# Two-block transformer kernel on one core: the experts' input is normalised in place and gathered by every fourth column, and two weight rows of layer 0 take the place of the reordered copy

## What is computed

```
x = layer_norm(ALPHA * x + m, ln1_g[layer], ln1_b[layer])
f = moe(x, w_router, b_router, moe_w1[layer], moe_w3[layer], moe_w2[layer])
x = layer_norm(ALPHA * x + f, ln2_g[layer], ln2_b[layer])

# moe: each token goes to 2 of 16 experts; for an expert e and its tokens xb
hb = jax.nn.silu(xb @ w1[e]) * (xb @ w3[e])
y  = hb @ w2[e]
```

## Time and profile before

| what | value |
| --- | --- |
| time, median of 3 runs | 2213.72 us (2211.26 to 2217.29) |
| profiled execution, its own time | 2218.69 us |
| its span | 2217.0 us |
| instructions in the profile | 27358 |
| TensorE matmul busy | 2137.2 us, 96% |
| VectorE / ScalarE / GpSimd busy | 1048.4 / 757.4 / 98.3 us |
| mean granted clock of TensorE | 0.995 |
| moved by DMA | 618.28 MB, 279 GB/s over the span |

### The profile page before, as it was taken

How to read it: one execution, slowest core, us unless ns; L and a number is a source line. 1 busy time by engine, 2 the same in 40 slices (tenths; PEclk the granted TensorE clock), 3 DMA queues, 4 the chain that set the end, 5 groups by cost and what they waited for, 6 DMA issues and landing times.

```text
span 2217.0 us, 27358 instructions
## 1 busy us (share of the span) xinstructions
PE 2137.2 (96%) x10936; PEld 1419.2 (64%) x10936; DVE 1048.4 (47%) x1570; ACT 757.4 (34%) x1085; POOL 98.3 (4%) x107
## 2 busy tenths in 40 slices
PE   8999999998999999998889999999999999989999
PEld 6653334333585344333268888878888888878887
DVE  5720000001482000000167778768778776866776
ACT  4622111100362111111043346653344335555332
POOL 3300000000000000000000003000000000300000
PEclk9999999999999999999999999999999999989999
DMA  8599999999949999999975554245555554415551
GB/s 288 216 394 428 427 427 429 426 428 425 377 192 414 426 427 428 427 428 427 421 267 191 196 171 160 77 149 186 199 171 174 195 197 158 136 48 188 186 195 57
DMA packets 171255, 618.28 MB, mean 279 GB/s; under 512 B 7976, under 2 KB 116688, under 8 KB 147600
## 3 DMA queue, kind: packets, MB, share of 16 engines
q1 hardware_dynamic: 168688, 612.00, 71.3%
q0 software_dynamic: 2464, 4.84, 0.7%
HBM read 615.76 MB, written 1.05 MB: 278 GB/s over the span
## 4 chain that ended last, share of the span: by engine, by line
PE 77%; DMA 11%; DVE 5%; ACT 4%; DVEq 1%; SPq 1%; issue 1%; ACTq 0%
PE W L2225 22%; PE W L2487 12%; PE W L2488 6%; DMA moe_split<-in_moe_w 4%; PE acc L2087 4%; PE acc L2091 4%; PE acc L2088 4%; PE W L2059 3%; PE W L2061 3%; PE W L2060 3%; DMA moe_own<-in_moe_w 3%; PE W L2207 2%; DMA moe_raw<-in_moe_w 2%; DMA moe_xt<-in_moe_w 2%; PE acc L2216 2%; PE W L2491 2%
## 5 line engine op out<-in xcount | busy, mean ns | idle before, releaser
L1329 DVE TENSOR_TENSOR w_lo<-raw,w_hi 128x2048 fp32r<-128x2048 f32 (+2 forms) x198 | 433.8, 2194 | 158.6 <-ACT w_hi L830 150.2
L830 ACT ACTIVATE w_hi<-raw 128x2048 fp32r<-128x2048 f32 (+2 forms) x203 | 372.2, 1833 | 304.2 <-PE acc L2091 134.1
L2487 PE MATMUL W<-xT_both,w_hi 128*128 128x512 f32 x1218 | 438.0, 399 | 3.9 <-DVE xT_both L1347 3.1
L1599 DVE TENSOR_TENSOR hid<-W,hid 128x512 f32<-128x512 f32 x32 | 22.1, 692 | 717.5 <-PE W L2225 717.4
L2488 PE MATMUL W<-xT_both,w_lo 128*128 128x256 f32 x1218 | 341.7, 281 | 0.0
L2487 PEld LDWEIGHTS W<-xT_both,w_hi 128*128 128x128 f32 x1218 | 229.2, 188 | 55.2 <-issue 3.7
L2488 PEld LDWEIGHTS W<-xT_both,w_lo 128*128 128x128 f32 x1218 | 230.1, 189 | 7.0
L2225 PE MATMUL W<-moe_split,xe 128*64 128x512 f32 x672 | 150.2, 595 | 9.1 <-DMA moe_split<-in_moe_w 9.1
L2225 PE MATMUL W<-moe_own,xe 128*64 128x512 f32 x608 | 138.2, 601 | 8.0 <-DMA moe_own<-in_moe_w 8.0
L2059 PE MATMUL W<-w_hi,xT_both 128*128 128x474 f32 (+1 forms) x376 | 145.4, 387 | 0.0
L2061 PE MATMUL W<-w_hi,xT_both 128*128 128x474 f32 (+1 forms) x376 | 142.7, 379 | 0.0
(11 more groups left out here) (420 smaller groups left out, 2959.2 us busy)
## 6 DMA issues: line engine op xcount, KB each, us to landing
moe_split<-in_moe_w SPq DMA_DIRECT2D x60, 2048.0 KB, 26.4
moe_raw<-in_moe_w SPq DMA_DIRECT2D x54, 2048.0 KB, 27.6
moe_own<-in_moe_w SPq DMA_DIRECT2D x50, 2048.0 KB, 25.8
raw<-in_ffn_w_gate SPq DMA_DIRECT2D x44, 1024.0 KB, 5.2
raw<-in_ffn_w_up SPq DMA_DIRECT2D x44, 1024.0 KB, 5.1
raw<-in_ffn_w_down SPq DMA_DIRECT2D x44, 1024.0 KB, 4.9
moe_xt<-in_moe_w SPq DMA_DIRECT2D x18, 2048.0 KB, 30.5
raw<-in_w_in SPq DMA_DIRECT2D x32, 948.0 KB, 4.8
```

Of the source, the lines that this page charges most:

```text
L830: s.activation(part(w_hi[split_slot(c)], cols), part(raw[slot_of(c)], cols), ACT.Copy).then_inc(hi_ready, 1)
L1329: v.tensor_tensor(part(w_lo[split_slot(c)], cols), part(raw[slot_of(c)], cols), part(w_hi[split_slot(c)], cols).bitcast(F32), ALU.subtract ...
L2487: t.matmul(wide, hi[:, cols], xT_both[:, kc].rearrange("p h t -> p (h t)"), start=(kc == 0), stop=False)
```

## The change

It drops the copy `xp`. ScalarE normalises x where it lies, with unit steps. `gather_pair` reads every fourth column of x as the stationary operand, and `normalise_x` has only gain and bias left. The 8 KB a partition at `region` are free in layer 0 until `lng` is loaded: rows 0 and 1 of chunk 8 (the ninth, `MOE_REGION`) are fetched to them (`region_rows`), and rows 0 and 1 of chunk 18 go into chunk 8's slot when chunk 8's other two rows do. In layer 1 the ring runs as before.

```
-        xp = nc.alloc_sbuf_tensor_at("xp", [P, TB, D], F32, offset=region)
+        region_rows = nc.alloc_sbuf_tensor_at("region_rows", [P, 2, D], F32, offset=region)
...
-                if m == MOE_AHEAD:
+                if layer == 0 and m == MOE_REGION:
+                    sp.dma_start(dst[:, 2:4], src[:, 2:4]).then_inc(moe_landed[slot], 16)
+                    sp.dma_start(dst[:, 0:2], weight_rows(layer, m + MOE_SLOTS)[:, 0:2]).then_inc(region_in, 16)
+                elif layer == 0 and m == MOE_REGION + MOE_SLOTS:
+                    sp.dma_start(dst[:, 2:4], src[:, 2:4]).then_inc(moe_landed[slot], 16)
+                elif m == MOE_AHEAD:
...
                 fetch_free_rows(layer)
                 if layer == 0:
+                    sp.dma_start(region_rows[:], weight_rows(layer, MOE_REGION)[:, 0:2]).then_inc(region_in, 16)
                     sp.wait_ge(lo_ready, last_split(second))
...
-                    last = s.activation(xp[:, b].rearrange("q (h k p) -> q h k p", h=MOE_Q, k=MOE_ROWS),
-                                        x[:, b].rearrange("q (h p k) -> q h k p", h=MOE_Q, k=MOE_ROWS), ACT.Identity,
-                                        bias=nmr[:, b:b + 1], scale=rstd[:, b:b + 1])
+                    last = s.activation(x[:, b], x[:, b], ACT.Identity, bias=nmr[:, b:b + 1], scale=rstd[:, b:b + 1])
...
-                        v.scalar_tensor_tensor(x[:, b, :], x[:, b, :], mv[:, b, 0:1], lng[:], ALU.subtract, ALU.mult)
+                        v.tensor_tensor(x[:, b, :], x[:, b, :], lng[:], ALU.mult)
...
-                        v.scalar_tensor_tensor(x[:, b, :], x[:, b, :], rstd[:, b:b + 1], lnb[:], ALU.mult, ALU.add)
+                        v.tensor_tensor(x[:, b, :], x[:, b, :], lnb[:], ALU.add)
...
-                        last = t.matmul(W[:, bank, j * P:(j + 1) * P].rearrange("p (a t) -> p a t", a=2), xp[:, b, kc * P:(kc + 1) * P],
+                        last = t.matmul(W[:, bank, j * P:(j + 1) * P].rearrange("p (a t) -> p a t", a=2), every_fourth(x[:, b], kc),
...
+                    if layer == 0 and m == MOE_REGION:
+                        pe.wait_ge(region_in, 32)
+                        pe.wait_ge(moe_landed[m % MOE_SLOTS], moe_count(layer, m))
+                        for k in range(2):
+                            row_halves(bank, stationary, MOE_ROWS * q + k, region_rows[:, k, 0:512], region_rows[:, k, 512:])
+                        for k in range(2, MOE_ROWS):
+                            last = halves(bank, stationary, MOE_ROWS * q + k, moe_ring[m % MOE_SLOTS], k * D)
+                        return last.then_inc(moe_used, 1)
```

More of the change, by code:

```diff
@@ L51 @@
 MOE_AHEAD = 5
+MOE_REGION = 8
 MOE_OWN = 3
@@ L390, in build_program @@
         ahead_in = sem("ahead_in")
+        region_in = sem("region_in")
         rope_in = sem("rope_in")
```

## The result

The change made the kernel slower: median 2241.05 us against 2215.07 us on the same chip (four runs each), ratio 1.0126 with a 95% interval from 1.0111 to 1.0140. That is 26.0 us more, where 2.0 us less was forecast. The profiled execution of the changed kernel has a span of 2239.5 us.

The account below looks back on a forecast made before the run. The prediction took the stream of weights to bound each layer's experts. Its terms, -2.46 us for the MB ahead and +0.4 for the gather, gave about -2.0 us: 2213.7 to 2211.7 us, range 2207.5 to 2217.5.

Parts of the forecast that it names:

- What bounds the kernel: Experts of both layers: the weight stream, not TensorE, sets each layer's end; 49.5 us of weight transfers in layer 0's chain.
- One MB more ahead: Layer 0's weight stream: 1 MB fetched in an idle DMA stretch makes chunks after chunk 18 land earlier; -2.46 us.
- Does a new hole open in the stream?: Layer 0's stream at chunk 20: no new hole, 2.1 us of cover left; cost 0, at most 2.46 us.
- The gather with a step of four: TensorE's gather: reading x in steps of four costs +6 ns a record, +0.4 us for both layers together.
- the upper bound: TensorE's gather: rival with the strided load exposed in full, 68 ns a record, TensorE the bound; 2223 us, chance 0.05.
- ScalarE's row: ScalarE's strided copy to `xp`: rival that TensorE's gather pays the same 2.3 times, 0.144 us more a record; 2262 us, chance 0.03.
- TensorE's slack: TensorE's DMA waits in the experts: room for 13.6 us more work in layer 0 and 11.5 in layer 1.
- The first gather ahead of chunk 0: 32 gather records ahead of chunk 0 delay chunk 10's issue: 0.2 us in layer 0, at most that in layer 1.
- ScalarE, VectorE, SyncE: Unit-step ScalarE activations of about 0.96 us, two-input VectorE operations, two more SyncE issues of 0.3 to 0.4 us: 0 each.

## Why the prediction was wrong

- **What bounds the kernel** held: the stream ended each layer before, and every experiment that slowed it or TensorE moved as that says.
- **One MB more ahead**: the transfer was issued where forecast and filled the idle stretch, and without the step it gave 1.5 to 2.0 us instead of 2.46. The mechanism was right and the size a little off.
- **Does a new hole open in the stream?** I put it at 0, with 2.1 us of cover at chunk 20. A partial one opened there, 0.9 to 1.0 us. Chunk 19 landed at 185.9 us (175.22 + 10.7), some 2.2 us after data of chunk 20 should have started (182.12 + 1.6), so the cover was there as I had counted it, and the rate fell all the same. A transfer that has not landed yet doesn't show that the stream is at full rate.
- **The gather with a step of four is the step that failed.** I took +6 ns a record from the pace of `hid`'s transposes, and put +68 ns as the upper bound, the whole difference between two transposes' loads. It is 122 ns ((7.73 - 3.84) / 32). The row was of the wrong operation: the earlier trace rows show a transpose, and a transpose pays 3 to 12 ns a record at steps of 2, 4 and 8, where the float32 product that the gather is pays 121 at a step of 4. The nearest row in form, same engine and same step, was not the nearest in kind, and the bound taken from it was no bound. ScalarE's row, of another engine, was the better guide: 144 ns, to which I gave 0.03. That it came so near is partly luck: the changed kernel's unit-step activations of the same 1024 elements took 1.23 us, so ScalarE's factor is 2204 / 1226 = 1.8 and not 2.3, and would have given 89 ns. The unknown should have stood open between both.
- **TensorE's slack** was too small in my account. 31.2 us of gather a layer ((7.73 - 3.84) + 14 x (3.93 - 1.98)), less the growth of 14.15 and 11.33 us, makes 17.0 and 19.9 us, where the listed DMA waits gave 13.6 and 11.5. In layer 1 the list ended at 1110 us, and four waits behind that make 2.5 us more. Also, one chunk at 1059 us took 5.35 us instead of 3.65: behind a DMA wait of 2.0 us the granted clock was 0.50 from 1060 to 1063 us, the lower level (1.2 GHz); that hid under the stream. What is left is about 0.25 us a wait in both layers. Products that follow each other overlap in their records: in the changed kernel a chunk starts 3.48 us after the one before it (511.40 - 507.92), while the records of 16 products last 3.65. Ahead of a wait that overlap is missing, so a listed wait understates what it leaves free. That is 0.17 of the 0.25 us; the rest is not shown. The two errors have opposite signs: with 122 ns and my slack the sum would have been 62.4 - 25.1 = +37 us.
- **The first gather ahead of chunk 0** is on the stream's path, as forecast, with some 1.5 us of cover. In the changed kernel it doesn't matter, since TensorE sets the end.
- **ScalarE, VectorE, SyncE** cost nothing, as forecast: the kernel with the in-place part alone has ratio 1.0000. The activations took 1.2 us each rather than 0.96. SyncE's issue to the free place took 1.14 us instead of 0.3 to 0.4, in a pause of 10 us, so it is not seen in the time.

## What to carry to other kernels

Before an operand's step is changed, ask what a load touches and what product hides it: at a step of four float32 elements the load of 128 columns takes twice as long as a product of 128 columns, and nothing of that is seen with 512. Take its price from the same operation at that step, and if the trace has none, leave the range open to other engines' rows. Slack is spent silently: half of the strided records, or an eighth in the wrong place, cost 5 to 6 us here, and all of them 26.

## What the hardware showed that I had not expected

- A transpose's load goes at 0.109 to 0.121 us at steps of 1, 2, 4 and 8, a float32 product's at 0.112, 0.118, 0.233 and 0.238. A product gives two records where a transpose gives one, and by its line price (1.82 ns) each of its loads costs as much as two reads of the kind a transpose makes (at most 0.121 / 128 = 0.95 ns a line at step 4). That it reads twice is a guess that no run here tests.
- The stream of 2 MB chunks moved 427 to 428 GB/s in pieces of 16 KB a partition, 423 with w1 and w3 (two thirds of it) in pieces of 8 KB, and 415 with them in pieces of 4 KB.
